# A planner's TensorE prices, per-head deadlines and a delay for cache rows, in a decoder layer with an expert layer

## The chip, the cores and the metric

One core of one Trainium2 chip runs the whole layer as one hand-written program. The metric is the device time of one execution in microseconds; the median of three runs of the kernel before is 3883.09 us (3873.05 to 3890.93).

Engines: PE is TensorE (matrix multiplies), PEld its weight loads, DVE VectorE, ACT ScalarE, POOL GpSimd, which here only issues indirect DMAs, and SP SyncE, which issues all other DMAs. Each engine takes its instructions in the order in which they stand in its program, and an instruction whose semaphore is not there yet holds all that stand behind it.

## What is computed

One layer of a decoder, in float32, for 1024 prompt tokens (eight tiles of 128) and 8 sample tokens with caches of 1024 earlier rows:

```python
q_a, k_a, v_a, q_b, k_b, v_b = project(x, pos, attn_norm, w_in)      # 1024 -> 2304, rope
o_a = banded_attention(q_a, k_a, v_a, sink)                          # 8 heads, window 128
o_b = combine_dilations(three dilated branches)                      # 8 heads
x = x + concat(rms_norm(o_a), rms_norm(o_b)) @ w_out
h = rms_norm(x, ffn_norm)
q = (h @ w_q).reshape(tokens, 8, 2, 128)                             # peer_ffn
s1, i1 = top_k(q[..., 0] . sub_keys, 16); s2, i2 = top_k(q[..., 1] . sub_keys, 16)
top_s, eid = top_k(all sums s1 + s2, 16)                             # 16 of 16384 experts per head
act = gelu(einsum('cd,chkd->chk', h, u[eid]))                        # gathered rows of peer_u
y = x + einsum('chk,chkd->cd', softmax(top_s) * act, v[eid])         # gathered rows of peer_v
```

The sample tokens attend to gathered cache rows. The caches, moved by one row, are outputs too. Each token needs 8 x 16 = 128 rows of `peer_u` and 128 of `peer_v`, of 4 KB each. That is 2048 gathers of 128 rows (512 KB) for the prompt, and it is most of what the kernel moves.

## The kernel before, in words

**Two kinds of work share the engines.** The base work is all that is dense: projection (`z`, `ze`, `zt`, `zv`), attention (`s`, `sm`, `se`, `p`, `pe`, `v`, `vd`, `vo`), norms, output projection (`o`, `ox`, `os`, `on`, `oh`, `ht`, `hv`), the query product and key scores of the expert layer (`q`, `qe`, `k`, `ke`), and the ranking of a head (`r0` to `r3`, `ge`, `gd`), where `r3` writes the 16 row numbers of a head to `idx` (L2084). The sample's attention has stages of its own: `smul` multiplies and reduces keys (L2122, L2124), twice for each of the 8 tokens, and `spv` multiplies values on PE (L1567 to L1569).

The other kind is the walk over the experts. It has 1058 places. At place p POOL gathers row number p of u for 128 tokens into a ring of four buffers (`u_ring`, L1350), and for the place 18 back (`LAG`) a row of v into another ring of four (`v_ring`, L1355). DVE takes the dot product of the u rows with h (L2204). After 16 places a head is complete: DVE and ACT make its 16 weights. A v row is then weighed and added up either on PE, where ACT first writes a diagonal matrix `diag` (L1832) and PE multiplies it with `v_ring` into `acc` (L1594), or on DVE (L2244). A ring's buffer is free when its dot product, or its weighing, is done. Places 0 to 1023 belong to the tiles 0 to 7, 128 each, and the head h of tile t starts at place 128 t + 16 h; the sample's 8 places come last.

**Groups.** Tiles are worked in groups (0), (1, 2), (3, 4), (5, 6), (7 and the sample). While a group is ranked, the next one is projected and attends; the output projection of a group lies between such phases. Weights stream through `wbuf`, four buffers of 1 MB, again for each group.

**The order of the work** is made when the program is built. `times_of(s)` gives each stage its engines and times in us. `merged` interleaves the queues of a phase by their summed times into one list, `BASE`. The class `Planner` then walks through time: it has the picks (dot, weigh and so on) and the stages of each engine in order, and takes at each step what can begin first. `ready_stage` says when a stage's inputs are there. `deadlines` gives each stage a place by which it is due (`by`): a stage that is due goes before a pick, one that isn't goes after. `load` and `send` choose for each v row whether PE or DVE weighs it. What comes out are only orders: `PLAN_OF` for PE, ACT and DVE, `PLAN_SP` for SP, and `ON_PE`. No time of the table is in the program itself; every wait is on a semaphore.

**SP and the sample's rows.** `sample_keys(r)` waits for the `smul` of token r - 1 and issues six DMAs into the one buffer (`s_k`, `s_kA`, `s_q`); `sample_values(r)` waits for the `spv` of r - 1 and issues four. So the rows of a token are asked for only when the token before is done.

Of the kernel before, what the change touches and what calls it, by code (L numbers as in the profile page):

```python
# [213 lines left out]
def pick_v(p):  # L214
    return pick_u(p - LAG) if p >= LAG else None
# [30 lines left out]
def times_of(s):  # L246
    kind, a, b = s[:3]
    sample = SAMPLE in (a, b) if kind in ("ze", "z") else a == SAMPLE
    n = a + 1 if kind in ("s", "sm", "se", "p", "pe", "v") else 0
    first = n == 1  # L250
    group = GROUPS[a] if kind in ("q", "qe", "k", "ke", "ge", "gd") else ()
    if kind == "z":
        return (("PE", 1.9 if a[0] == "kva" else 3.6),)
    if kind == "ze":
        return (("ACT", 0.7),) + ((("DVE", 1.7),) if a != "vb" else ())
    if kind == "o":
        return (("PE", 7.2),)
# [38 lines left out]
BASE = [s for phase in PHASES for s in merged(phase)]  # L296
AT = {s[:3] + tuple(s[6:7]): n for n, s in enumerate(BASE)}
# [95 lines left out]
ENGINES = ("PE", "ACT", "DVE")  # L393
HOP = 0.15
PACE = 2.9


class Planner:
# [51 lines left out]
    def deadlines(self):  # L450
# [4 lines left out]
        marks = [(self.given[0, 0], 0)]  # L455
        for t in ORDER[1:]:
            p = [p for p in range(PLACES) if pick_u(p) is not None and tile_of(pick_u(p)) == t][0]
            n = self.given[t, 0]
            if n > marks[-1][0]:
                marks.append((n, max(p - 10, 1)))  # L460

        total = [sum(cost[:n + 1]) for n, _ in marks]
        i = 0
        self.by = [0.0] * (marks[0][0] + 1)
        while i + 1 < len(marks):
# [5 lines left out]
            i = j  # L471
# [12 lines left out]
    def pick_line(self, e):  # L484

        out = []
        for p in range(PLACES):
# [9 lines left out]
            elif e == "ACT":  # L497
                out += [("tanh", ended, 0.3)] if ended is not None else []
                out += [("diag", p, 0.42)] if pick_v(p) is not None and pick_v(p)[0] == "f" else []
                out += [("fsq", final, 1.3)] if final is not None else []  # L500
            else:
                out += [("weigh", p, 1.98)] if pick_v(p) is not None else []
        return out

    def ready_stage(self, e):
# [3 lines left out]
        n, i, _ = self.parts[e][self.base[e]]  # L509
# [1900 lines left out]
```

How the kernel before makes its waits and increments, by code:

```python
        def need(eng, s, n):  # L777
            if n > 0:
                eng.wait_ge(s, n)
# [242 lines left out]
            def load_weights(b, i):  # L1023
                kind, g, part = W_LOADS[b][i]
                if i:
                    was, wg, wpart = W_LOADS[b][i - 1]
                    if was == "in":
                        sp.wait_ge(z_mm, Z_PARTS[wpart, IN_GROUPS[wg][-1]])
                    elif was == "out":
                        sp.wait_ge(o_mm, 2 * OI[GROUPS[wg][-1]] + wpart[0] + 1)
                    else:
                        sp.wait_ge(q_mm, 16 * wg + 2 * (wpart + 1))
                    if kind == "out" and g == LAST and part[0] == 0:
                        sp.wait_ge(s_fold, 1)
                if kind == "in":
                    c, half = part
                    w = COLS[c][1]
                    c0 = KD * sum(COLS[x][1] for x in CHUNKS[:CHUNKS.index(c)]) + 4 * w * half
                    sp.dma_start(wbuf[:, b, 0:4 * w], w_in[:, c0:c0 + 4 * w]).then_inc(wt_in[b], 16)
                elif kind == "out":
                    c0 = 4096 * part[0] + 2048 * part[1]
                    sp.dma_start(wbuf[:, b, :], w_out[:, c0:c0 + 2048]).then_inc(wt_in[b], 16)
                else:
                    sp.dma_start(wbuf[:, b, :], w_q[:, 2048 * part:2048 * (part + 1)]).then_inc(wt_in[b], 16)
# [14 lines left out]
            def load_x(kind, t):  # L1059
# [5 lines left out]
                    else:  # L1065
                        sp.wait_ge(o_h, OI[wt] + 1)
                        sp.wait_ge(x2_out[wt], 16)
                R = rows_of(t)
```

## Time and profile before

| | us |
|---|---|
| median of three runs | 3883.09 |
| lowest, highest | 3873.05, 3890.93 |
| the profiled execution | 3865.63 |
| its span, first to last instruction | 3863.8 |

| engine | busy us | share of the span |
|---|---|---|
| PE | 2715.3 | 70% |
| DVE | 2532.2 | 66% |
| POOL | 2339.2 | 61% |
| ACT | 631.4 | 16% |

The 16 DMA engines moved 1295.70 MB, of which the gathers are 1086.46 MB. No engine is full over the span, so what counts is where the DMA engines stand idle, and who let them. The profile is one execution, some 17 us shorter than the median of the runs.

### The profile page before, as it was taken

The numbers are of one execution on the slowest core, as the hardware profiler recorded it, in microseconds if no ns is written. First come the engines' busy times: TensorE is split into PE (matmuls) and PEld (weight loads), VectorE is DVE, ScalarE is ACT, GpSimd is POOL, SyncE is SP. The second block draws the span as 40 slices with busy tenths as digits, with TensorE's granted clock in tenths as the row PEclk, the third lists the DMA queues.
The fourth block names the chain that finished last, engine by engine and source line by source line (L and its number), as shares of the span: only waits on it lengthen the run. The fifth ranks groups of instructions, "written<-read, shape, count | busy, mean of one in ns | idle before, by whom it ended". The sixth has DMA issues, their size and how long they took to land.

```text
span 3863.8 us, 30640 instructions
## 1 busy us (share of the span) xinstructions
PE 2715.3 (70%) x7286; PEld 1323.9 (34%) x7286; DVE 2532.2 (66%) x6330; ACT 631.4 (16%) x1880; POOL 2339.2 (61%) x2076
## 2 busy tenths in 40 slices
PE   5866669687778777777798785457766566665665
PEld 3533335343434344334344343122332222222221
DVE  1467777677766677767667876555787555555553
ACT  2112212122211121212111121001111011110110
POOL 0155644476465577776745775444667777777774
PEclk7877879788899888888999888678987988888887
DMA  9799889899789899998988998777999999999997
GB/s 365 269 365 335 311 334 345 328 349 347 259 311 357 342 344 357 344 351 316 352 332 300 361 358 311 275 259 259 363 353 354 368 374 367 376 360 377 365 372 251
DMA packets 344554, 1295.70 MB, mean 335 GB/s; under 512 B 41880, under 2 KB 44784, under 8 KB 330912
## 3 DMA queue, kind: packets, MB, share of 16 engines
q0 software_dynamic: 298368, 1086.46, 76.2%
q1 hardware_dynamic: 46008, 207.29, 14.2%
q8 instruction: 61, 1.00, 0.1%
q14 instruction: 117, 0.96, 0.1%
HBM read 1272.76 MB, written 55.43 MB: 344 GB/s over the span
## 4 chain that ended last, share of the span: by engine, by line
POOL 24%; PE 24%; DMA 23%; issue 12%; DVE 9%; DVEq 3%; another core or an unknown queue 2%; ACT 1%; SPq 1%; ACTq 0%; POOLq 0%
DMA v_ring<-in_peer_v,idx 13%; POOL v_ring L1355 12%; POOL u_ring L1350 12%; PE acc L1594 12%; PE pS L1400 4%; DMA u_ring<-in_peer_u,idx 4%; PE pA L1526 3%; DMA wbuf<-zS_scr 2%; DVE u_ring L2204 2%; PE pS L1503 1%; DVE accs L2244 1%; DMA xbuf<-in_x_all 1%; PE pS L1442 1%; DMA o_all<-in_cache_swa 1%
## 5 line engine op out<-in xcount | busy, mean ns | idle before, releaser
L1594 PE MATMUL acc<-v_ring,diag 128*128 128x512 f32 x2820 | 1662.0, 733 | 861.0 <-DMA v_ring<-in_peer_v,idx 728.1
L1355 POOL DMA_INDIRECT v_ring<-in_peer_v,idx x1024 | 1191.3, 1163 | 772.3 <-PE acc L1594 355.4
L2204 DVE CUSTOM_DVE_ANT_0 u_ring<-u_ring,hb 128x1024 f32<-128x1024 f32 x1024 | 1244.7, 1222 | 577.8 <-DMA u_ring<-in_peer_u,idx 554.8
L1350 POOL DMA_INDIRECT u_ring<-in_peer_u,idx x1024 | 1123.5, 1097 | 713.3 <-issue 292.5
L1594 PEld LDWEIGHTS acc<-v_ring,diag 128*128 128x128 f32 x2820 | 605.5, 230 | 1748.6 <-issue 1603.1
L2244 DVE SCALAR_TENSOR_TENSOR accs<-v_ring,wv,accs 128x1024 f32<-128x1024 f32 x319 | 409.8, 1285 | 89.1 <-DMA v_ring<-in_peer_v,idx 57.4
L1832 ACT ACTIVATE diag<-idn,wv 128x128 f32<-128x128 f32 x705 | 264.8, 396 | 1160.1 <-PE acc L1594 818.9
L1400 PE MATMUL pS<-wbuf,T 128*128 128x512 f32 (+1 forms) x640 | 263.5, 562 | 22.7 <-DVE T L1927 16.0
L1526 PE MATMUL pA<-T,wbuf 128*128 128x256 f32 (+2 forms) x1280 | 256.4, 357 | 21.3 <-issue 15.6
L1526 PEld LDWEIGHTS pA<-T,wbuf 128*128 128x128 f32 x1280 | 221.2, 204 | 72.8 <-issue 46.6
L1400 PEld LDWEIGHTS pS<-wbuf,T 128*128 128x128 f32 x640 | 123.0, 197 | 142.7 <-issue 129.5
L1503 PE MATMUL pS<-wbuf,T 128*128 128x512 f32 (+1 forms) x288 | 131.4, 612 | 6.9 <-DVE xbuf L2000 4.4
L1442 PE MATMUL pS<-KTB,qT 64*128 64x512 f32 (+3 forms) x176 | 84.1, 591 | 58.2 <-DMA qT<-qT_scr 41.3
L1823 ACT ACTIVATE gl<-gl 128x16 f32<-128x16 f32 (+1 forms) x65 | 14.0, 215 | 642.7 <-DVE gl L2222 402.4
L1972 DVE CUSTOM_DVE_ANT_0 S<-pS,maskB 128x256 f32<-128x256 f32 (+6 forms) x56 | 46.2, 825 | 83.7 <-PE pM L1444 79.1
L1706 ACT ACTIVATE S<-S,anm 128x128 f32<-128x128 f32 (+7 forms) x64 | 49.5, 774 | 303.3 <-DVE anm L1979 248.9
L1479 PEld LDWEIGHTS pM<-VB,PT 128*128 128x128 f32 x560 | 79.5, 213 | 33.8 <-issue 22.4
L2204 DVE DVE_READ_ACCUMULATOR2_ANT dots<- 128x1 f32 x1024 | 84.1, 82 | 0.0
L1479 PE MATMUL pM<-VB,PT 128*128 128x64 f32 x560 | 78.2, 293 | 7.7 <-ACT PT L1642 6.7
L1503 PEld LDWEIGHTS pS<-wbuf,T 128*128 128x128 f32 (+1 forms) x288 | 53.2, 187 | 81.8 <-issue 81.8
L1941 DVE TENSOR_TENSOR onehot<-qT,rcs 128x64 f32<-128x64 f32 (+3 forms) x36 | 7.6, 212 | 102.2 <-ACT qT L1642 100.7
L1462 PE MATMUL pT<-idn,S 128*128 128x128 f32 x280 | 48.3, 311 | 36.8 <-ACT aden L1708 29.3
(224 smaller groups left out, 1908.4 us busy)
## 6 DMA issues: line engine op xcount, KB each, us to landing
wbuf<-in_w_in SPq DMA_DIRECT2D x40, 1024.0 KB
wbuf<-in_w_q SPq DMA_DIRECT2D x40, 1024.0 KB
out_dil_s<-in_cache_dil SPq DMA_DIRECT2D x8, 4092.0 KB
wbuf<-in_w_out SPq DMA_DIRECT2D x20, 1024.0 KB
u_ring<-in_peer_u,idx POOLq DMA_INDIRECT x1024
v_ring<-in_peer_v,idx POOLq DMA_INDIRECT x1024
xbuf<-in_x_all SPq DMA_DIRECT2D x16, 512.0 KB
wbuf<-in_w_in SPq DMA_DIRECT2D x10, 512.0 KB
```

The source lines that it names most:

```text
L1350: pool.indirect_dma_start(u_ring[:, entry % RU, :], None, table, bass.IndirectOffsetOnAxis(rows, 0))\
L1355: pool.indirect_dma_start(v_ring[:, entry % RV, :], None, peer_v, bass.IndirectOffsetOnAxis(rows, 0))\
L1400: m = pe.matmul(pS[0:R, 512 * (i % 2):512 * (i % 2) + w], xT[t][:, 4 * half + k, :], wbuf[:, b, k * w:(k + 1) * w], start=(half == 0 and k ...
L1442: pe.matmul(pS[:, b0 * P:b1 * P], qT[rows, q, 4 + p, :], KTB[rows, p, b0 * P:b1 * P], start=True, stop=True)
L1479: pe.matmul(pM[:, 0:64], PT[:, k, :], VB[:, k, cols], start=(k == 0), stop=(k == blocks_of(t) - 1))
L1503: m = pe.matmul(pS[0:R, half * 512:(half + 1) * 512], hT[g][:, k, columns(t)], wbuf[:, b, k % 4 * 512:(k % 4 + 1) * 512], start=(k == 0), ...
L1526: m = pe.matmul(pA[:, 0:width_of(GROUPS[g])], wbuf[:, b, k * 256 + i % 2 * P:k * 256 + (i % 2 + 1) * P], hT[g][:, k, :], start=(k == 0), s ...
L1594: m = pe.matmul(acc[0:R, half * 512:(half + 1) * 512], w, v_ring[:, entry % RV, half * 512:(half + 1) * 512], start=first, stop=last, skip ...
L1706: act.activation(B, B, ACT.Exp, bias=anm[:, b, 0:1], accum_out=aden[:, b, 0:1])
L1832: act.activation(diag[:, i % 4, :], idn[:, :], ACT.Copy, scale=wv[:, section % 2, v[1] % TOPK:v[1] % TOPK + 1]).then_inc(d_set, 1)
L2204: dve.tensor_tensor_reduce(row, row, hb[:, t % 2, :], 1.0, 0.0, ALU.mult, ALU.add, dots[:, section % 2, j:j + 1]).then_inc(u_used, 1)
L2244: dve.scalar_tensor_tensor(accs[:, i % 2, :], v_ring[:, e % RV, :], wv[:, section % 2, j:j + 1], accs[:, i % 2, :], ALU.mult, ALU.add).the ...
```

## The change

The diff touches the planner alone; no instruction of any engine has another form, and POOL issues the same gathers in the same order. It does five things.

1. `times_of`: the times of all PE stages are smaller, most of them by a factor of 1.1 to 2.8 (a product of the projection 3.6 to 2.0, of the output 7.2 to 4.0, of the queries of two tiles 4.0 to 2.1), and the weighing of a v row on PE goes from 1.98 to 1.25. Times of DVE and ACT stay.
2. `deadlines`: every head of a tile has its own mark; before, only head 0 of each tile had one.
3. `ready_stage`: a first part of `smul` and each `spv` can begin 12 us (`FETCH`) after the one before is done.
4. `ready_stage`: `r3` waits for the end of the tile that had the same `idx` slot.
5. `SLOTS`, `SLOT` and `width_of` are defined earlier.

```diff
@@ times_of @@
     if kind == "z":
-        return (("PE", 1.9 if a[0] == "kva" else 3.6),)
+        return (("PE", 1.1 if a[0] == "kva" else 2.0),)
...
-        "q": (("PE", 3.4 if len(group) == 1 else 4.0),), "qe": (("ACT", 0.36),), "k": (("PE", 0.45 * len(group)),),
+        "q": (("PE", 1.2 if width_of(group) < 2 * P else 2.1),), "qe": (("ACT", 0.36),), "k": (("PE", 0.2 * len(group) + 0.1),),
...
+FETCH = 12.0
...
@@ Planner.deadlines @@
-            n = self.given[t, 0]
-            if n > marks[-1][0]:
-                marks.append((n, max(p - 10, 1)))
+            for h in range(HEADS if t != SAMPLE else 1):
+                n = self.given[t, h]
+                if n > marks[-1][0]:
+                    marks.append((n, max(p + TOPK * h - 10, 1)))
...
@@ Planner.pick_line @@
-                out += [("weigh", p, 1.98)] if pick_v(p) is not None else []
+                out += [("weigh", p, 1.25)] if pick_v(p) is not None else []
...
@@ Planner.ready_stage @@
+        if BASE[n][0] in ("smul", "spv") and BASE[n][2] == 0:
+
+            m = n - 1 if BASE[n][0] == "spv" or BASE[n][1] == 0 else AT["smul", BASE[n][1] - 1, 1]
+            if BASE[n][0] == "spv" and BASE[n][1] == 0:
+                m = AT["smul", NS - 1, 1]
+            if BASE[n][0] == "spv" and BASE[n][1] > 0:
+                m = AT["spv", BASE[n][1] - 1, 0]
+            end = self.part_end.get((m, 0))
+            if end is None:
+                return None
+            ready = max(ready, end + FETCH)
+        if BASE[n][0] == "r3":
+
+            for t in BASE[n][6]:
+                if OI[t] >= SLOTS and ("fsum", ORDER[OI[t] - SLOTS]) not in self.ends:
+                    return None
```

In the changed kernel all lines below the planner stand 18 further down (L2204 is L2222, L1594 is L1612). Three places show what the new orders are.

**DVE, the sample's keys.** L2122 and L2124 are the multiply and reduce of `smul`, L2204 a dot product of the walk (two rows each), L2244 a weighing. Before, from the second part of one token's `smul` to the first part of the next:

```order
L2122 TENSOR_TENSOR wbuf<-o_all,wbuf 128x512
L2124 TENSOR_REDUCE PT<-wbuf 128x8
L2204 ISA u_ring,dots<-u_ring,hb 128x1024
L2204 ISA dots 128x1
L2244 SCALAR_TENSOR_TENSOR accs<-v_ring,wv,accs 128x1024
L2204 ISA u_ring,dots<-u_ring,hb 128x1024
L2204 ISA dots 128x1
L2122 TENSOR_TENSOR wbuf<-wbuf 128x1024
```

After, the end of such a stretch (it begins with one more dot product; L2102 writes the row numbers of a head):

```order
L2102 SCALAR_TENSOR_TENSOR idx<-sel 128x2x16
L2222 ISA u_ring,dots<-u_ring,hb 128x1024
L2222 ISA dots 128x1
L2262 SCALAR_TENSOR_TENSOR accs<-v_ring,wv,accs 128x1024
L2222 ISA u_ring,dots<-u_ring,hb 128x1024
L2222 ISA dots 128x1
L2222 ISA u_ring,dots<-u_ring,hb 128x1024
L2222 ISA dots 128x1
L2140 TENSOR_TENSOR wbuf<-wbuf 128x1024
```

Before, two places of the walk lie between one token's end and the next token's start (none to two in all such stretches); after, it is four to six. The sample's whole attention lies over the places 596 to 652 before and 452 to 561 after.

**DVE, the row numbers of head 5 of tiles 1 and 2**, of which POOL needs the first at place 208. L2084 writes them, L2217 closes the head before. Before:

```order
L2065 TENSOR_REDUCE sel<-onehot 128x32
L2084 SCALAR_TENSOR_TENSOR idx<-sel 128x2x16
L2089 TENSOR_REDUCE gsum<-gexp 128x2
L2091 RECIPROCAL gsum<-gsum 128x2
L2093 TENSOR_TENSOR gates<-gexp,gsum 128x2x16
L2204 ISA u_ring,dots<-u_ring,hb 128x1024
L2204 ISA dots 128x1
L2217 TENSOR_TENSOR gl<-dots 128x16
```

After, at the same closing of a head:

```order
L2083 TENSOR_REDUCE sel<-onehot 128x32
L2222 ISA u_ring,dots<-u_ring,hb 128x1024
L2222 ISA dots 128x1
L2235 TENSOR_TENSOR gl<-dots 128x16
L2236 SCALAR_TENSOR_TENSOR gl<-dots,gates 128x16
L2238 TENSOR_SCALAR gl<-gl 128x16
L2240 TENSOR_TENSOR gl<-gl,dots 128x16
```

Before, 208 dot products stand ahead of the write; after, 169 do, and the write is gone from here. For the heads 4 to 7, needed at the places 192, 208, 224 and 240, the writes stand behind 191, 208, 224 and 240 dot products before, and behind 144, 169, 191 and 211 after. The last head of all is ranked at place 746 before and at 643 after.

**PE, the projection of tiles 5 and 6.** L1400 x4 of 512 columns is one projection stage, L1526 x8 one query stage, L1416 a transpose, L1594 x2 one weighing. Before:

```order
L1400 MATMUL pS<-wbuf,T 128x512 x4
L1594 MATMUL acc<-v_ring,diag 128x512 x2
L1526 MATMUL pA<-T,wbuf 128x256 x8
L1400 MATMUL pS<-wbuf,T 128x512 x4
L1594 MATMUL acc<-v_ring,diag 128x512 x4
L1400 MATMUL pS<-wbuf,T 128x512 x4
L1594 MATMUL acc<-v_ring,diag 128x512 x2
```

After:

```order
L1612 MATMUL acc<-v_ring,diag 128x512 x4
L1418 MATMUL pS<-wbuf,T 128x512 x4
L1434 MATMUL pT<-idn,qT 128x128
L1544 MATMUL pA<-T,wbuf 128x256 x8
L1418 MATMUL pS<-wbuf,T 128x512 x4
L1434 MATMUL pT<-idn,qT 128x128
L1418 MATMUL pS<-wbuf,T 128x512 x8
L1612 MATMUL acc<-v_ring,diag 128x512 x2
```

Before, one or two base stages lie between weighings; after, five big ones do. Over the whole program PE weighs 713 v rows before and 789 after, DVE 319 and 243; of the first 120 places DVE weighs 54 before and 24 after.

## Rows read from the trace of the kernel before

**Rows 1.** Busy time by stretch, granted clock, DMA share and GB/s.

```profile
core 0: us, PE busy (x) PEld busy (x) DVE busy (x) ACT busy (x) POOL busy (x), PEclk, DMA share, GB/s
162.00:600.00 438.00, 298.45 (x993) 173.57 (x992) 315.06 (x878) 89.86 (x292) 225.73 (x200) 0.80 0.91 338
...
1200.00:1900.00 700.00, 538.48 (x1565) 279.19 (x1565) 513.42 (x1309) 140.45 (x407) 484.12 (x413) 0.88 0.93 342
...
2300.00:2760.00 460.00, 280.40 (x650) 118.50 (x651) 277.07 (x626) 51.92 (x159) 238.85 (x211) 0.77 0.82 293
...
2960.00:3760.00 800.00, 504.42 (x833) 184.54 (x834) 459.99 (x769) 83.02 (x230) 615.86 (x560) 0.84 0.98 368
```

**Rows 2.** u gathers issued in two stretches, counted: x, ns min/median/max, first and last.

```profile
L1350 POOL DMA_INDIRECT u_ring<-in_peer_u,idx x61: 932/938/1974, 2371.4 to 2683.7; - x61
...
L1350 POOL DMA_INDIRECT u_ring<-in_peer_u,idx x280: 933/937/2167, 2961.1 to 3759.9; - x140
```

**Rows 3.** The page: GB/s moved in each of 40 slices.

```profile
GB/s 365 269 365 335 311 334 345 328 349 347 259 311 357 342 344 357 344 351 316 352 332 300 361 358 311 275 259 259 363 353 354 368 374 367 376 360 377 365 372 251
```

**Rows 4.** POOL's waits over the span: us in total, times, longest.

```profile
POOL v_ring L1355 <- PE acc L1594: 366.1, 164, 24.4
...
POOL u_ring L1350 <- DVE idx L2084: 218.7, 5, 161.5
POOL u_ring L1350 <- DVE dots L2204: 202.0, 68, 14.0
POOL v_ring L1355 <- DVE accs L2244: 133.9, 35, 14.4
```

**Rows 5.** Around one token's keys: start, us, instruction, [idle before]; DVE, then SP.

```profile
2389.57 0.69 DVE L2124 TENSOR_REDUCE PT<-wbuf 128x8 f32<-128x512 f32 x1
...
2405.02 1.23 DVE L2122 TENSOR_TENSOR wbuf<-wbuf 128x1024 f32<-128x1024 f32 x1 [11.10 <-DMA wbuf<-zS_scr]
...
2392.91 0.65 SPq L1187 DMA_DIRECT2D wbuf<-zS_scr  x1
```

**Rows 6.** DVE's wait for the sample's keys over the span.

```profile
DVE wbuf L2122 <- DMA wbuf<-zS_scr: 70.6, 8, 12.7
```

**Rows 7.** POOL, the sample's stretch, the first and the last of nine.

```profile
2386.69 1.68 POOL L1355 DMA_INDIRECT v_ring<-in_peer_v,idx  x1 [14.40 <-DVE accs L2244]
...
2651.54 1.15 POOL L1355 DMA_INDIRECT v_ring<-in_peer_v,idx  x1 [21.98 <-PE acc L1594]
```

**Rows 8.** POOL in order of time, where it lacked row numbers.

```profile
983.95 0.94 POOL L1350 DMA_INDIRECT u_ring<-in_peer_u,idx  x1 [19.08 <-DVE idx L2084]
...
1048.53 0.94 POOL L1350 DMA_INDIRECT u_ring<-in_peer_u,idx  x1 [19.59 <-DVE idx L2084]
...
1107.26 0.94 POOL L1350 DMA_INDIRECT u_ring<-in_peer_u,idx  x1 [13.19 <-DVE idx L2084]
```

**Rows 9.** The page's group of DVE's weighings.

```profile
L2244 DVE SCALAR_TENSOR_TENSOR accs<-v_ring,wv,accs 128x1024 f32<-128x1024 f32 x319 | 409.8, 1285 | 89.1 <-DMA v_ring<-in_peer_v,idx 57.4
```

**Rows 10.** PE's groups by shape: records, busy us, mean ns, idle before.

```profile
L1594 PE MATMUL acc<-v_ring,diag 128*128 128x512 f32 x2820 | 1662.0, 733 | 861.0 <-DMA v_ring<-in_peer_v,idx 728.1 <-ACT diag L1832 86.6 <-issue 45.2
L1400 PE MATMUL pS<-wbuf,T 128*128 128x512 f32 x512 | 230.4, 599 | 6.7 <-DMA wbuf<-in_w_in 4.2 <-ACT qT L1642 2.4
L1526 PE MATMUL pA<-T,wbuf 128*128 128x256 f32 x768 | 184.5, 395 | 6.8 <-issue 3.7 <-ACT sc L1642 3.1
L1503 PE MATMUL pS<-wbuf,T 128*128 128x512 f32 x256 | 117.3, 615 | 6.9 <-DVE xbuf L2000 4.4 <-ACT T L1642 2.5
...
L1513 PE MATMUL pT<-idn,S 128*128 128x128 f32 x64 | 11.1, 332 | 25.2 <-DVE S L2010 25.2
```

**Rows 11.** Two stretches with the granted clock, as in rows 1.

```profile
200.00:400.00 200.00, 125.59 (x427) 75.50 (x428) 140.29 (x406) 45.88 (x158) 106.16 (x97) 0.74 0.91 339
...
1200.00:1300.00 100.00, 91.59 (x247) 45.82 (x248) 72.45 (x210) 15.78 (x40) 56.20 (x48) 0.97 0.95 361
```

More of the change, by code:

```diff
@@ L41 @@
 SC_SLOTS = 4
+SLOTS = 5
+SLOT = {t: i % SLOTS for t, i in OI.items()}
 PLACE_IN_GROUP = {t: s for g in GROUPS for s, t in enumerate(g)}
@@ L68, in rows_of, with width_of @@
     return NS if t == SAMPLE else P
+def width_of(group):
+    return sum(rows_of(t) for t in group)
 def prompt_of(group):
@@ L260, in times_of @@
     return {
-        "xg": (("DVE", 2.7),), "zt": (("PE", 0.5 if a == "kva" else 1.8),),
+        "xg": (("DVE", 2.7),), "zt": (("PE", 0.3 if a == "kva" else 0.8),),
         "zv": (("ACT", 0.35 if a == "kva" else 0.65),),
-        "s": (("PE", 0.8 if first else 0.6 + 0.25 * n),), "sm": (("DVE", 1.9 if first else 1.3 + 0.14 * n),),
-        "se": (("ACT", 1.4 if first else 1.3 + 0.12 * n),), "p": (("PE", 0.9 if first else 0.8 + 0.4 * n),),
-        "pe": (("ACT", 0.5 if first else 0.9 + 0.12 * n),), "v": (("PE", 0.7 if first else 0.7 + 0.3 * n),),
+        "s": (("PE", 0.6 if first else 0.6 + 0.13 * n),), "sm": (("DVE", 1.9 if first else 1.3 + 0.14 * n),),
@@ L266, in times_of @@
+        "se": (("ACT", 1.4 if first else 1.3 + 0.12 * n),), "p": (("PE", 0.6 if first else 0.5 + 0.18 * n),),
+        "pe": (("ACT", 0.5 if first else 0.9 + 0.12 * n),), "v": (("PE", 0.5 if first else 0.5 + 0.14 * n),),
         "vd": (("DVE", 0.6),), "vo": (("ACT", 0.6),),
-        "n1": (("ACT", 1.5),), "n2": (("DVE", 2.9),), "n3": (("ACT", 1.3),), "nt": (("PE", 3.3),), "ng": (("ACT", 2.4),),
+        "n1": (("ACT", 1.5),), "n2": (("DVE", 2.9),), "n3": (("ACT", 1.3),), "nt": (("PE", 1.6),), "ng": (("ACT", 2.4),),
@@ L272, in times_of @@
         "ge": (("ACT", 0.3),), "gd": (("DVE", 0.9),),
-        "sin": (("DVE", 2.2),), "smul": (("DVE", 2.7 if b == 0 else 1.6),), "ssc": (("PE", 1.6),),
-        "ssm": (("DVE", 2.6),), "sse": (("ACT", 1.2),), "ssd": (("DVE", 1.5),), "spr": (("PE", 1.5),),
-        "spe": (("ACT", 1.0),), "spv": (("PE", 2.4),), "sod": (("DVE", 2.0),), "sfo": (("PE", 1.8),),
+        "sin": (("DVE", 2.2),), "smul": (("DVE", 2.7 if b == 0 else 1.6),), "ssc": (("PE", 1.0),),
+        "ssm": (("DVE", 2.6),), "sse": (("ACT", 1.2),), "ssd": (("DVE", 1.5),), "spr": (("PE", 1.0),),
@@ L276, in times_of @@
+        "spe": (("ACT", 1.0),), "spv": (("PE", 2.1),), "sod": (("DVE", 2.0),), "sfo": (("PE", 1.1),),
         "so": (("DVE", 1.3),), "sr0": (("DVE", 3.4),), "sr1": (("DVE", 2.4),), "sr2": (("DVE", 1.5),), "sr3": (("DVE", 2.7),), "sge": (("ACT", 0.3),),
@@ L714 @@
 STAGED = {x: i for i, x in enumerate(x for x in Z_ITEMS if x[0] in ("qa", "qb") and 0 < x[1] < NT)}
-SLOTS = 5
-SLOT = {t: i % SLOTS for t, i in OI.items()}
 R3 = [s for s in BASE if s[0] == "r3"]
 RANKED = {(t, s[2]): i + 1 for i, s in enumerate(R3) for t in s[6]}
-def width_of(group):
-    return sum(rows_of(t) for t in group)
 X_LOADS = (("sq", 0), ("sq", 1), ("sq", 2), ("o", 0), ("sq", 3), ("sq", 4), ("o", 1), ("o", 2), ("sq", 5), ("sq", 6),
```

4 lines of the change are left out of this document (2 added, 2 removed).

## The prediction, as it was put on record

> **What bounds the kernel now.** I read the GB/s of the slices first, then busy time by stretch, then what POOL waited for, since POOL issues the gathers that are most of the traffic. From 2960 us on, when all base work is over, the DMA engines are busy for 0.98 of the time at 368 GB/s [rows 1], and 280 places pass in 800 us, 2.857 us each [rows 2]. That stretch is bound by DMA alone, and no order of the engines can shorten it. Earlier the same engines move 338, 342 and, around the sample's attention, 293 GB/s [rows 1]; the slices show the same dip, 311 275 259 259 [rows 3]. The bytes are the same whatever the order. So the kernel's time is its bytes at about 368 GB/s plus the time in which the DMA engines are starved, and POOL's waits tell who starves them: PE's weighings, DVE's dot products and weighings, and row numbers that come late [rows 4]. It follows that moving base work to earlier places is worth nothing by itself: a place that goes without base work later costs its 2.857 us all the same. Only starved time can be won, and only new starved time can be lost.
>
> **Part 1, the sample's cache rows.** In the order before, at most two places lie between the end of one token's `smul` and the start of the next. The trace shows what the rows take: the reduce ends at 2390.26, SP's last request goes out at 2392.91, and the next multiply begins at 2405.02 after 11.10 us of idling on DVE [rows 5]; 14.8 us from end to start. Over eight tokens DVE idles 70.6 us for them [rows 6], dot products and weighings stand behind it, both rings fill, and POOL pauses. Nine such pauses of over 6 us, from the first to the last shown [rows 7], add up to 122.7 us; the last two are PE waiting for the value rows in the same way. What is it worth? The places 600 to 660 took 312 us [rows 2]. Undisturbed they cost 60 x 2.857 = 171 us, and the sample's own rows, some 13 MB, another 13/0.368 = 36 us. 312 - 171 - 36 = 105 us starved. By rates instead: 460 us at 293 GB/s are 135 MB, 394 us at the 342 of the stretch 1200 to 1900 [rows 1], a gain of 66 us. After the change four to six places lie between, 11.4 to 17.1 us at 2.857, against the 14.8 measured; SP's order has nothing new in between. Some stretches will still be short by up to 3 us, which a ring of four buffers (11.4 us) swallows. I take **-95 us**, bounds -105 to -66.
>
> **Part 2, deadlines per head.** Before, the numbers of the heads 5, 6 and 7 of tile 1 are written on DVE only after all the dot products that stand before them, and POOL, which runs ahead of DVE, waits 19.08, 19.59 and 13.19 us for them [rows 8], 51.9 us. The first of the five waits of that kind, 161.5 us [rows 4], is the start of the kernel and stays: 136 instead of 138 base stages stand ahead of it. After the change 28 places or more lie between a head's write and its need, from head 0 of tile 1 on. The gain can't be more than 51.9 us; in the slices there the rate is 259 and 311 [rows 3], so some traffic of SP used the gaps. I take **-45**, bounds -52 to -32.
>
> **Part 3, more weighings on PE.** 76 go from DVE to PE, 30 of them in the first 120 places. That takes 30 x 1.285 = 39 us [rows 9] from a DVE that is busy for 315 of the first 438 us [rows 1]. There POOL waits for DVE more than for PE. On PE a weighing has 4 records: 1662.0/705 = 2.36 us [rows 10], and 30 x 2.36 = 71 us come in where PE is busy for 298 of 438. I take **-15**, bounds -39 to 0. In the places without base work DVE has room and this is worth nothing.
>
> **Part 4, PE's new prices.** Counted by stage, the trace gives 230.4/64 = 3.6 us for a projection stage (8 records), 184.5/48 = 3.84 for a query stage (16), 117.3/16 = 7.3 for half an output product (16), and 11.1/8 = 1.4 for the eight transposes of a tile [rows 10]. The old table has 3.6, 4.0, 7.2 and 3.3, the new one 2.0, 2.1, 4.0 and 1.6. So the new table is right for transposes, and for products it has little more than half of what this trace shows; a weighing is 1.25 against 2.36, or 1.7 with the clock at its upper level. The planner therefore lays product stages on PE closer than they fit. In the rows of PE's order five big stages stand between two weighings: 3.6 + 3.84 + 3.6 + 7.2 and two small transposes, 18.7 us. Four v buffers cover 4 x 2.857 - 1.7 = 9.7 us; behind that POOL stops. Priced so, 18 stretches between weighings exceed the cover, by 98 us together, nearly all at three spots where one group's output product meets the next projection (places 80 to 120, 200 to 240, 360 to 400). Before, 9 such stretches exceeded it, by 26 us, and one long stretch in which DVE did the weighing. But DMA has weights to load at these spots, so starved time is less: over 80 to 119, 200 to 239 and 360 to 399 PE has 215, 212 and 222 us of work, DMA 193, 193 and 189 (40 places at 2.857 and the weights), an excess of 74 us; before, it was 8. A dense PE also gets its higher clock, 0.97 at 92% busy against 0.74 in the stretch 200 to 400 [rows 11], so the stages there cost some 5% less than the mean. I take **+45**, bounds 0 to +98.
>
> **Part 5, between these spots.** From place 240 to 360 and 400 to 440 the base work of PE rises by some 5 us in 20 places (57 us), DVE's stays. PE was 77% busy in 1200 to 1900 [rows 1] and would be near 85%. I take **+10**, bounds 0 to +40. The `r3` rule for `idx` slots binds nowhere near: the tiles in question end over 100 places before the write.
>
> A page of the notes speaks on part 4: the Trainium skill, "Perfetto Trace Analysis", section "Tensor Engine Instruction (MATMUL, LD_WEIGHTS)", says that a matmul's recorded end is estimated from its size and not observed. If PE's records overstate, the new table may be nearer the truth; that is the second rival. Against it stands that busy time per stage counts back-to-back records by their starts, not by the last end.
>
> **The sum.** 3865.6 (the profiled execution) - 95 - 45 - 15 + 45 + 10 = 3765.6. The median of the runs is 17.5 us above the profiled execution, so 3783.
>
> **Rivals.** (a) *The delay is too short.* 12 us stands against 14.8 measured, and SP's requests queue behind gathers. If half of part 1 stays, 3783 + 48 = 3831. For it: five places at 2.857 are 14.3 us. Against it: a miss of 1 to 3 us, not 11, and rings that cover it. (b) *PE's prices are good enough.* Parts 4 and 5 cost nothing, parts 1 to 3 give -95 - 52 - 25: 3865.6 - 172 + 17.5 = 3711. For it: PE stands idle 728 us waiting for v rows [rows 10], room that a dense order could use. Against: that idling lies elsewhere. (c) *PE becomes the bound and the kernel slower.* The place is the three spots; the price is each stretch between weighings that outlasts 9.7 us. The 18 hold 273 us of stages; at the clock of 0.74 instead of some 0.86 they hold 317, 142 more than their cover. With +40 of part 5 and gains of only 66 and 32: 3865.6 + 142 + 40 - 98 + 17.5 = 3967. It decides once the uncovered time passes the 98 to 155 us of gains. Against it speaks the clock that rises with density. (d) *The two cancel*: the orders change as planned, and what is won at the sample is lost at the spots, about 3883. That the delay or the deadlines did nothing is excluded by the orders themselves.
>
> **Chances.** Forecast 0.55, (b) 0.17, (a) 0.11, (d) 0.07, (c) 0.10. A difference of 0.5%, 19 us, is about what measurements of this kernel can tell. Faster by more: the first three, less a little for (a) with less gain elsewhere, 0.80; within 0.10; slower 0.10. The range 3700 to 3880 leaves out (c), most of (d) and the best ends of all bounds at once.
>
> **What would show it.** Part 1: DVE's wait for the keys under 25 us and no POOL pause over 6 us from the sample's rows, the dip to 259 gone. Part 2: no wait of POOL for `idx` but the first. Part 3: shorter waits of POOL for DVE before 600 us. Part 4: POOL's wait for PE's `acc` grows, with pauses of 5 to 10 us bunched at three spots, and PE over 90% busy there. The stretch without base work must still show 2.857 us a place. The prediction is wrong if the DMA rate outside the sample's part falls below that of before, or if new waits of DVE for PE's results stand in front of dot products.

## The result and the profile after

The changed kernel took 3931.86 us (median of 4 runs, 3921.03 to 3942.17) where the kernel before, run beside it, took 3878.14: a ratio of 1.0133, 95% interval 1.0093 to 1.0173. It is slower by some 52 us; the forecast was 100 us faster. The profiled execution has a span of 3919.2 us.

The page's GB/s in 40 slices, which answer to [rows 3]; three holes have replaced the old dips:

```profile
GB/s 362 263 316 347 301 298 262 320 314 343 341 274 191 339 350 360 354 282 212 306 353 370 374 368 386 282 313 348 368 368 368 365 369 366 371 359 377 357 372 258
```

Busy time by stretch, columns as in [rows 1]. The first three lines are the places 80 to 119, 220 to 239 and 360 to 399, the fourth the places 200 to 219, the fifth the places 402 to 525 with the sample's keys, the last the stretch without base work:

```profile
475.00:732.00 257.00, 210.40 (x669) 116.49 (x668) 148.13 (x491) 53.19 (x146) 87.51 (x80) 0.91 0.78 280
1079.00:1269.00 190.00, 147.23 (x486) 86.20 (x485) 90.52 (x329) 34.03 (x86) 41.87 (x41) 0.87 0.67 234
1651.00:1894.00 243.00, 207.21 (x625) 102.63 (x623) 140.47 (x445) 43.29 (x114) 83.29 (x80) 0.91 0.73 255
...
1011.00:1079.00 68.00, 57.06 (x146) 25.61 (x144) 52.37 (x135) 13.25 (x38) 47.88 (x41) 0.95 0.93 331
...
1900.00:2300.00 400.00, 281.78 (x719) 131.28 (x720) 302.31 (x690) 67.72 (x193) 281.29 (x248) 0.85 0.98 361
...
2960.00:3760.00 800.00, 508.78 (x852) 183.24 (x852) 447.16 (x737) 85.66 (x236) 595.64 (x557) 0.85 0.98 367
```

The same places 80 to 119, 200 to 239 and 360 to 399 in the kernel before:

```profile
455.00:655.00 200.00, 155.19 (x470) 86.06 (x471) 143.69 (x409) 34.71 (x96) 93.74 (x82) 0.87 0.90 335
...
941.00:1107.00 166.00, 120.55 (x394) 66.53 (x393) 125.32 (x361) 38.84 (x123) 89.47 (x80) 0.85 0.77 281
1545.00:1668.00 123.00, 94.60 (x289) 50.88 (x288) 95.04 (x236) 30.36 (x88) 92.37 (x80) 0.85 0.95 347
```

The stretch without base work is unchanged (367 GB/s against 368). The three spots took 257 + 258 + 243 = 758 us instead of 200 + 166 + 123 = 489, 269 more. By the times at which POOL issues its u gathers, the rest of the walk took less: the places 120 to 200 and 240 to 360 lost 7 and 55 us, 400 to 580 lost 51, 580 to 660 lost 83 and 660 to 1020 lost 35, while the first 80 took 21 us more. The sum is some 58 us. What was gained at the sample and what came back for base work moved ahead did not pay for the spots. By the rows above not all of the 269 us is starved time. Time times GB/s gives 201 MB moved in the three spots after and 156 before: some 45 MB, mostly the weights of base work that now stands there, are 121 us at 368 GB/s, and other places no longer have to move them. Time times the idle share of DMA gives 191 us starved after and 64 before, 127 more. The two make 248 of the 269. Both are estimates from rounded rows of one execution each.

POOL's waits over the span, which answer to [rows 4] (us in total, times, longest):

```profile
POOL v_ring L1373 <- PE acc L1612: 483.1, 193, 18.6
POOL u_ring L1368 <- DVE dots L2222: 342.0, 78, 15.4
...
POOL u_ring L1368 <- DVE idx L2102: 160.5, 1, 160.5
...
POOL v_ring L1373 <- DVE accs L2262: 25.4, 19, 3.2
```

DVE's wait for the sample's keys, which answers to [rows 6]:

```profile
DVE wbuf L2140 <- DMA wbuf<-zS_scr: 6.5, 4, 2.9
```

So the change did at its own places what it should: row numbers are waited for only at the start (218.7 us in five waits, now 160.5 in one), the sample's keys cost 6.5 us instead of 70.6, and waiting for DVE's weighings falls from 133.9 to 25.4. But waiting for PE's weighings grew by 117 us and for DVE's dot products by 140. Pauses of POOL over 6 us, without the first wait for row numbers, add up to 437 us (42 of them; before, 350 in 30), and 311 us of them (29 pauses) lie in the three spots.

What holds DVE's dot products up shows in DVE's own waits, for the x rows and for PE's attention scores (`pM`). Before, then after:

```profile
DVE S L1972 <- PE pM L1444: 79.1, 21, 15.3
...
DVE xbuf L2000 <- DMA xbuf<-in_x_all: 6.9, 1, 6.9
```

```profile
DVE S L1990 <- PE pM L1462: 135.3, 32, 15.5
...
DVE xbuf L2018 <- DMA xbuf<-in_x_all: 61.8, 4, 18.6
```

**Inside one spot.** The chain of waits through the places 220 to 239 shows three parts (start, us, what; x is a count of records):

```profile
1083.98 15.37 DMA xbuf<-in_x_all
1099.38 1.23 DVE xbuf L2018
...
1107.26 1.30 DVE S L2028
1108.60 1.97 PE pT L1531 x8
...
1111.79 6.11 PE pA L1544 x16
1117.90 1.72 PE acc L1612 x4
...
1174.40 1.72 PE acc L1612 x4
1176.11 3.43 PE pS L1418 x8
...
1179.99 10.30 PE pS L1418 x24
1190.29 3.45 PE pA L1544 x16
1193.75 1.72 PE acc L1612 x4
...
1218.94 5.90 DMA qT_scr<-qT
1224.90 5.88 DMA qT<-qT_scr
1230.82 2.93 PE pS L1460 x4
...
1239.82 3.36 PE acc L1612 x4
```

The same three parts by busy time:

```profile
1083.00:1108.00 25.00, 5.60 (x20) 2.57 (x18) 7.43 (x19) 2.81 (x6) 5.81 (x6) 0.70 0.82 319
1111.00:1218.00 107.00, 105.73 (x337) 61.94 (x338) 58.55 (x221) 18.57 (x44) 21.21 (x21) 0.97 0.73 252
1218.00:1268.00 50.00, 29.41 (x109) 17.76 (x107) 20.13 (x78) 11.55 (x33) 10.46 (x9) 0.76 0.44 144
```

First, 28 us in which the end of one group's output product stands in a row: DVE waits for the x rows, adds them, normalizes, PE transposes, and only then can the queries begin. Then 107 us in which PE is 99% busy with projection, queries and weighings. Last, 50 us of attention, with a round trip of q through memory (11.8 us) and then PE, DVE and ACT by turns; the DMA engines are busy for 0.44 of it. In all three, dot products and weighings stand in line behind other stages, and POOL has no free buffer. PE and DMA don't idle in the same parts. PE idles for some 20 us in the entry and 21 in the attention and for 1 in between. The DMA engines idle for 5 us in the entry, where the x rows come behind two blocks of weights, for 29 in the dense part and for 28 in the attention.

### The profile page after: what moved, and what is told of

It reads as the page before. It is cut to its first block, busy times and chain, and to the rows that moved or that the text cites. A ratio compares the mean times of both kernels' runs of the same rounds, so it can differ in the third digit from the quotient of the medians.

```text
span 3919.2 us, 31248 instructions
## 1 busy us (share of the span) xinstructions
PE 2815.0 (72%) x7590; PEld 1347.1 (34%) x7590; DVE 2433.2 (62%) x6254; ACT 664.2 (17%) x1956; POOL 2275.0 (58%) x2076
## 4 chain that ended last, share of the span: by engine, by line
PE 30%; POOL 23%; DMA 19%; issue 14%; DVE 7%; DVEq 2%; ACT 2%; another core or an unknown queue 1%; SPq 0%; ACTq 0%; POOLq 0%
PE acc L1612 13%; POOL v_ring L1373 12%; POOL u_ring L1368 11%; DMA v_ring<-in_peer_v,idx 11%; PE pS L1418 6%; PE pA L1544 4%; PE pS L1521 3%; DMA xbuf<-in_x_all 2%; DMA u_ring<-in_peer_u,idx 2%; DVE u_ring L2222 2%; DMA wbuf<-zS_scr 1%; PE pS L1460 1%; DMA wbuf<-in_w_in 1%; DVE accs L2262 1%
## 5 line engine op out<-in xcount | busy, mean ns | idle before, releaser
L1612 PE MATMUL acc<-v_ring,diag 128*128 128x512 f32 x3124 | 1780.1, 712 | 780.6 <-DMA v_ring<-in_peer_v,idx 668.7
L2222 DVE CUSTOM_DVE_ANT_0 u_ring<-u_ring,hb 128x1024 f32<-128x1024 f32 x1024 | 1244.9, 1223 | 663.3 <-DMA u_ring<-in_peer_u,idx 617.0
L1373 POOL DMA_INDIRECT v_ring<-in_peer_v,idx x1024 | 1163.8, 1136 | 814.4 <-PE acc L1612 475.7
L1368 POOL DMA_INDIRECT u_ring<-in_peer_u,idx x1024 | 1086.3, 1061 | 795.3 <-DVE dots L2222 342.0
L1612 PEld LDWEIGHTS acc<-v_ring,diag 128*128 128x128 f32 x3124 | 650.7, 224 | 1767.7 <-issue 1652.1
L1850 ACT ACTIVATE diag<-idn,wv 128x128 f32<-128x128 f32 x781 | 296.0, 397 | 1307.4 <-PE acc L1612 760.1
L2262 DVE SCALAR_TENSOR_TENSOR accs<-v_ring,wv,accs 128x1024 f32<-128x1024 f32 x243 | 312.3, 1285 | 65.3 <-DMA v_ring<-in_peer_v,idx 35.4
L1418 PE MATMUL pS<-wbuf,T 128*128 128x512 f32 (+1 forms) x640 | 261.5, 558 | 20.3 <-DVE T L1945 15.4
L1990 DVE CUSTOM_DVE_ANT_0 S<-pS,maskB 128x256 f32<-128x256 f32 (+6 forms) x56 | 46.2, 825 | 150.4 <-PE pM L1462 135.3
L1497 PE MATMUL pM<-VB,PT 128*128 128x64 f32 x560 | 73.4, 280 | 19.9 <-ACT PT L1660 11.1
L2222 DVE DVE_READ_ACCUMULATOR2_ANT dots<- 128x1 f32 x1024 | 84.5, 83 | 0.0
L2018 DVE TENSOR_TENSOR xbuf<-xbuf,pS 128x1024 f32<-128x1024 f32 (+1 forms) x9 | 11.0, 1220 | 104.0 <-DMA xbuf<-in_x_all 61.8
```

Source lines behind the costliest of these rows:

```text
L1368: pool.indirect_dma_start(u_ring[:, entry % RU, :], None, table, bass.IndirectOffsetOnAxis(rows, 0))\
L1373: pool.indirect_dma_start(v_ring[:, entry % RV, :], None, peer_v, bass.IndirectOffsetOnAxis(rows, 0))\
L1418: m = pe.matmul(pS[0:R, 512 * (i % 2):512 * (i % 2) + w], xT[t][:, 4 * half + k, :], wbuf[:, b, k * w:(k + 1) * w], start=(half == 0 and k ...
L1497: pe.matmul(pM[:, 0:64], PT[:, k, :], VB[:, k, cols], start=(k == 0), stop=(k == blocks_of(t) - 1))
L1612: m = pe.matmul(acc[0:R, half * 512:(half + 1) * 512], w, v_ring[:, entry % RV, half * 512:(half + 1) * 512], start=first, stop=last, skip ...
L1850: act.activation(diag[:, i % 4, :], idn[:, :], ACT.Copy, scale=wv[:, section % 2, v[1] % TOPK:v[1] % TOPK + 1]).then_inc(d_set, 1)
```

## The experiments

Times are compared by ratio to the kernel before in runs of the same chip, since that kernel took 3845.55, 3831.14 and 3882.15 us in the three sets. The ratios and intervals are those on record; they differ from the quotient of the two medians by up to 0.4% (fetch_only: 0.986 against 0.982). Differences between two ratios are good to 0.5 to 1 per cent.

**times_only: the new PE prices alone, in the kernel before.** They take the place of the old ones in `times_of` and `pick_line`; deadlines and delay stay as they were.

```diff
-        return (("PE", 1.9 if a[0] == "kva" else 3.6),)
+        return (("PE", 1.1 if a[0] == "kva" else 2.0),)
...
-                out += [("weigh", p, 1.98)] if pick_v(p) is not None else []
+                out += [("weigh", p, 1.25)] if pick_v(p) is not None else []
```

> The kernel before with only the new PE prices (stages and weighing); marks of head 0 alone, no delay for cache rows. Theory A, the new prices squeeze base work into a few spots and the squeeze is what costs: the loss is all here and the gain at the sample is missing, so about 3932 + 95 = 4027 us, 3980 to 4060, with places 80 to 120 and one later pair of projections at 5 to 9 us a place, and POOL pauses at the sample's rows as before. Rival B, the prices are harmless and deadlines or delay did the harm: 3850 to 3890.

Measured: 3951.89 us, ratio 1.030 (1.0221 to 1.0379). The prices alone make the kernel slower, by more than the whole change. On the scale of the first chip the ratio is 3994 us, in the range of theory A, though only 1.6% (some 65 us) above the changed kernel where 95 were expected. The three spots took 265, 249 and 253 us. Its slices show the spots in new places and the sample's stall, which nothing cured here (228 to 293):

```profile
GB/s 358 266 332 339 310 283 261 302 285 329 336 305 192 340 355 329 361 277 191 326 357 293 251 228 291 370 367 379 377 376 373 369 370 396 406 378 386 387 390 270
```

**old_times: the changed kernel with all old PE prices.** The reverse edit in the changed kernel; per-head deadlines, delay and the `r3` rule stay.

> The changed kernel with the old PE prices (stages and weighing); deadlines per head, delay and idx rule stay. Theory A: the gains of parts 1 and 2 without the squeeze, 3878 - 95 - 45 = 3738 us, 3715 to 3780; no stretch of 20 places over 6 us a place. Rival B: about 3932, 3900 to 3950.

Measured: 3726.95 us, ratio 0.972 (0.9645 to 0.9796). The prices are therefore worth 1.0133/0.972 = 1.042, or 160 us, in the changed kernel, and all that the change cost comes from them. No 20 places, counted in twenties from 0, took over 5.9 us each. Waiting for v rows to be weighed fell from 483.1 to 396.3 us, for dot products from 342.0 to 201.1, and the places 220 to 239 took 62 us (columns as in [rows 1]):

```profile
1028.00:1090.00 62.00, 51.30 (x129) 22.56 (x129) 49.39 (x140) 12.89 (x39) 45.21 (x41) 0.92 0.93 341
```

**fetch_only and heads_only: each cure alone, in the kernel before.**

```diff
+FETCH = 12.0
...
+            ready = max(ready, end + FETCH)
```

> The kernel before with only the delay of 12 us for the sample's keys and values. Theory A: part 1 alone, 3878 - 95 = 3783 us, 3773 to 3812 by its bounds; DVE's wait for the keys falls from 70.6 us to under 25. If half of the stall stays because the rows take 14.8 us and not 12: about 3830. If the DMA engines were not starved there at all: 3878.

Measured: 3774.74 us, ratio 0.9857 (0.9784 to 0.9929).

```diff
+            for h in range(HEADS if t != SAMPLE else 1):
+                n = self.given[t, h]
...
+                    marks.append((n, max(p + TOPK * h - 10, 1)))
```

> The kernel before with only a mark per head in the deadlines. Theory A: part 2 alone, 3878 - 45 = 3833 us, 3826 to 3846; POOL's waits for idx are gone but the first. If the time in those waits was used by other traffic: 3865 to 3880.

Measured: 3817.69 us, ratio 0.9934 (0.9895 to 0.9972). By the times, each fell between its theory A and the rival value (0.973 to 0.983 and about 0.988 for fetch_only, 0.987 to 0.992 and 0.997 or more for heads_only). By the traces each removed its own wait and left the other. fetch_only, POOL's and DVE's waits:

```profile
POOL u_ring L1362 <- DVE idx L2096: 223.2, 5, 161.0
...
DVE wbuf L2134 <- DMA wbuf<-zS_scr: 8.3, 4, 2.8
```

heads_only, the same two waits:

```profile
POOL u_ring L1351 <- DVE idx L2085: 161.7, 2, 161.4
...
DVE wbuf L2123 <- DMA wbuf<-zS_scr: 88.2, 8, 14.0
```

Alone they give 1.4% and 0.7%, together 2.8%. The surplus of 0.7% lies within the intervals, so the times alone don't show that it is more than the sum; the traces, of one chip, show how it can be. At place 580 heads_only stood at 2265 us and fetch_only at 2326: 61 us ahead. From 580 to 680, where the sample's attention lies in both, heads_only then took 487 us and fetch_only 327. Against the kernel before, whose trace is of another chip, heads_only was 48 us ahead at place 580 and 3 at place 680: its lead was used up in the sample's stall. In old_times most of the lead of the deadlines is kept (2284 at place 580, 334 us to 680). Against each other in spans, the delay on top of the deadlines is worth 3822.1 - 3732.5 = 90 us (83 by the ratios), the deadlines on top of the delay 3766.6 - 3732.5 = 34 us (53 by the ratios). The first lies close to the 95 forecast, the second on either side of 45.

**old_stages and old_weigh: which of the new prices does it.** In the changed kernel, old_stages has the stage times of the old table and 1.25 for a weighing; old_weigh has the new stage times and 1.98 for a weighing.

```diff
-                out += [("weigh", p, 1.25)] if pick_v(p) is not None else []
+                out += [("weigh", p, 1.98)] if pick_v(p) is not None else []
```

> The changed kernel with the stage times of the old table; a weighing on PE stays priced at 1.25, and the delay and the marks stay. It ranks the last head at place 742 (changed kernel: 643) and weighs 768 rows on PE (789). Theory S, the small prices of the base stages do the harm, since they pack base work into three spots where PE, ACT and DVE wait for one another: ratio to the kernel before 0.97 to 0.985, no 20 places over 7 us each, most of the way back to the 0.972 of old_times. Rival W, the price of a weighing does it, since more rows are weighed on PE and fewer on DVE: ratio 1.00 to 1.015, as the changed kernel, with long waits of POOL for PE's acc spread over all places with base work.

> The changed kernel with a weighing on PE priced at 1.98 again; the new small stage times, the delay and the marks stay. It ranks the last head at place 648 (changed kernel: 643) and weighs 763 rows on PE (789). Theory S (stage prices do the harm): ratio to the kernel before 1.005 to 1.02, with the places 220 to 240 at 8 us or more each. Rival W (the weighing's price does it): ratio 0.97 to 0.985. If both prices share the harm, this one and old_stages both land near 0.99.

Measured: old_stages 3718.79 us, ratio 0.9684 (0.9641 to 0.9726), no 20 places over 6.2 us each; old_weigh 3853.02 us, ratio 1.0064 (1.0025 to 1.0103), the places 220 to 239 at 8.3 us each. Theory S stands: the stage prices cost 1.0133/0.9684 = 1.046, the weighing's price 1.0133/1.0064 = 1.007, at the edge of what the two intervals tell. The traces put this last part at the start: the first 80 places took 293 us before, 314 in the changed kernel, 310 in times_only, and 297 and 293 in old_weigh and old_stages, so it takes both small prices. In orders that are spread out the 63 more weighings on PE (768 against 705) go with a ratio 0.4% lower, about 14 us, which these intervals can't tell from nothing.

**traced: PE prices as the trace of the kernel before shows them.** In the changed kernel (three of the changed lines; the other PE times and the weighing's 2.0 as in the expectation):

```diff
-        return (("PE", 1.1 if a[0] == "kva" else 2.0),)
+        return (("PE", 2.1 if a[0] == "kva" else 3.6),)
...
-        return (("PE", 4.0),)
+        return (("PE", 7.3),)
...
-FETCH = 12.0
+FETCH = 15.0
```

> The changed kernel with PE times as the trace of the kernel before shows them: projection stage 3.6 (kva 2.1), half an output product 7.3, query stage 3.84 (2.25 for one tile), transposes of a tile 1.4, s 0.7 + 0.24 n, v 0.6 + 0.28 n, a weighing 2.0, and a delay of 15 us. It ranks the last head at place 763. Theory S: with prices that fit what PE shows the planner leaves room for the chain of engines: ratio to the kernel before 0.965 to 0.975, equal to old_times or up to 0.7% faster, no 20 places over 6.5 us each. Rival D, the new deadlines pack the work and the prices hardly matter: 0.99 or more.

Measured: 3710.34 us, ratio 0.9664 (0.9616 to 0.9712). So it isn't new prices that hurt but small ones: prices taken from the trace are as good as the old ones, and no better within the intervals. (The delay went to 15 us in the same run, so the two aren't told apart here.)

**half_proj and half_proj_old: is PE full at the spots?** Both leave half of the projection's product out; q, k and v are therefore those of half the contraction. half_proj is made from the changed kernel, half_proj_old from old_times.

```diff
-                for k in range(4):
+                for k in range(2):
...
-                                  stop=(half == 1 and k == 3), skip_group_check=True)
+                                  stop=(half == 1 and k == 1), skip_group_check=True)
```

> The changed kernel with half of the projection's product left out: each projection stage on PE does 2 of its 4 blocks of the contraction (4 records of 512 columns instead of 8, some 1.7 us instead of 3.4); orders, transfers and all other stages stay. It tells what bounds the three spots. Theory P, PE is full there (99% busy from 1111 to 1218 us in the changed kernel): the places 220 to 240, 190 us with 64 us of projection records in them, take 150 to 165 us, the three spots together give back 70 to 100 us, ratio to the kernel before 0.985 to 0.995 (changed kernel 1.0133). Rival C, latency of the chain PE, ACT, DVE bounds the spots and PE's amount of work doesn't: the places 220 to 240 take 180 us or more, ratio 1.005 to 1.013.

> The same half of the projection's product left out of old_times (the changed kernel with the old PE times), as the control: the same PE work goes, but from orders in which it is spread. Theory P: PE is seldom full there, so little comes back, 0 to 25 us, ratio to the kernel before 0.965 to 0.972 (old_times 0.972). If PE work were worth its time everywhere, some 110 us would come back here too, and the ratio would be near 0.945.

Measured: half_proj 3871.32 us, ratio 0.9958 (0.9927 to 0.999); half_proj_old 3731.03 us, ratio 0.9621 (0.9582 to 0.966). In half_proj the places 220 to 239 took 171 us instead of 190, and the three spots gave back 49 us (690 to 641, with 220 to 239 counted for the second): between what the two theories expected. Its chain of waits through the same spot:

```profile
1061.46 15.64 DMA xbuf<-in_x_all
...
1089.55 5.17 PE pA L1544 x16
...
1177.88 6.85 DMA qT_scr<-qT
1184.78 5.61 DMA qT<-qT_scr
1190.43 2.93 PE pS L1460 x4
```

and busy time of its parts:

```profile
1090.00:1190.00 100.00, 78.08 (x258) 46.49 (x257) 58.73 (x219) 18.25 (x43) 24.78 (x24) 0.91 0.85 305
1190.00:1228.00 38.00, 29.03 (x109) 17.90 (x110) 19.50 (x77) 11.65 (x35) 5.82 (x7) 0.80 0.28 85
```

From the first query product to the round trip of q it takes 88 us (1089.55 to 1177.88), 107 in the changed kernel (1111.79 to 1218.94): all of the 19 us won lie here. PE's projection records fell by 27 us in the places 220 to 239, so not all of that came back; with less work PE waits in this part too (78 us busy of the 100 shown). The entry (28 us, from the request for the x rows) and the attention (50 us) are as long as before. So both theories hold, each for its part of the spot: 107 us of the 190 are bound by PE, 78 by transfers and stages that wait for one another, whatever PE has to do; 5 us lie ahead of the entry. In the control less came back: 1.0% against 1.75% by the ratios, and 10 us against 50 in the three times 40 places by the traces (456 to 446 us, 758 to 708). The 1.0% is 38 us where at most 25 were expected, but the intervals leave both open. How much of the 78 us would be covered if the same stages stood farther apart wasn't tried by itself; that old_times has no such hole says that most of it is. Nor was it tried to ask for the x rows ahead of the two blocks of weights. DVE's wait for them is 61.8 us in the changed kernel and 62.8 in half_proj, 41.9 in times_only and 40.3 in old_weigh, but at most 16.7 in every run with the old or the traced stage prices.

**old_fetch16, old_fetch20 and stages_fetch16: is the delay too short?** old_times with `FETCH` at 16 and 20, old_stages with 16.

```diff
-FETCH = 12.0
+FETCH = 16.0
```

> old_times (the changed kernel with all old PE times) with the delay for the sample's rows at 16 us instead of 12. Theory F, 12 us against 14.8 measured is covered by the rings: ratio within 0.4% of the 0.972 of old_times, and no pause of POOL over 6 us goes in the sample's part. Rival (a), the delay is too short: 0.960 to 0.967, since DVE's remaining wait for the keys goes away.

> old_times with the delay at 20 us (12: 0.972, 16: 0.965). If the rows still came late at 16: 0.958 to 0.963. If 16 covers the 14.8 us measured and more only drags the sample's attention out: 0.964 to 0.970.

> old_stages (the changed kernel with the old stage times and the new 1.25 for a weighing, 0.968) with the delay at 16 us. If the 0.7% that 16 us gave in old_fetch16 is real and adds up: 0.960 to 0.964, the fastest so far. If it was scatter between chips or between orders: 0.966 to 0.970.

Measured: old_fetch16 3705.79 us, ratio 0.9648 (0.9597 to 0.9698); old_fetch20 3741.53 us, 0.9645 (0.961 to 0.968); stages_fetch16 3770.89 us, 0.9709 (0.9666 to 0.9752). DVE's wait for the keys from `wbuf` is 11.8 us at 12, and at 16:

```profile
DVE wbuf L2140 <- DMA xbuf<-zS_scr: 3.8, 1, 3.8
...
DVE wbuf L2140 <- DMA wbuf<-zS_scr: 0.4, 1, 0.4
```

The wait goes as it should, but it was small. old_fetch16 came out at the number of rival (a), its sister stages_fetch16 the other way; the intervals overlap with those of 12. The three comparisons give 0.7% and 0.7% for more than 12 us and 0.2% against it, and the waits that went (15.3 us of waiting for keys at 12, 4.2 at 16) are 0.3%; a gain stays open. old_fetch16, old_fetch20 and traced are the fastest versions, some 3.5% below the kernel before, and not told apart from one another nor from old_stages.

## Why the prediction was wrong

- **Part 1** (95 us forecast): right where the deadlines are also in place, 90 us by the spans and 83 by the ratios; alone 1.4%, about 55. After the change DVE waits 6.5 us for keys (under 25 expected), the new stretch of the sample's keys moves 361 GB/s, and no pause over 6 us is left there. In fetch_only the stall itself is gone, 259 us for the places 580 to 659 instead of 371 (traces of two chips). It took 628 us from place 680 to 880 where heads_only took 580, but at 363 and 367 GB/s: these are transfers that were still due, and no new stall. Why its ratio shows only 55 us isn't settled by a run.
- **Part 2** (45): right with the delay in place, 34 to 53 us, and the four waits for row numbers are gone, as expected. Alone it showed only 0.7%, since part of its lead was lost in the sample's stall.
- **Part 3** (15): waits for DVE's weighings went down as expected (133.9 to 25.4 us), and before 600 us POOL waited 116 us for DVE instead of 143. But it waited 60 us for PE there instead of 22, and the first 80 places took 21 us more and not less: there the sign was wrong. In the spread-out orders of old_stages the gain is 0.4% at most, within its error.
- **Parts 4 and 5** (45 + 10): here the forecast failed. With part 3 the prices were put at +40; measured they are +160. The places were right and so was PE's work in them: 215, 212 and 222 us were forecast for the three times 40 places, 210, 204 and 207 were there. The place and the sign were rival (c)'s. The step that failed is the one that set the time of a spot to the larger of PE's work and DMA's. The time was 257, 258 and 243, that is 47, 54 and 36 us above PE's own work, because the dense part has an entry and an attention at its ends in which PE waits too, while the DMA engines idle in the dense part and the attention. That is shown in one spot, the places 220 to 239, and taken over to the other two. The starved time, for which I had 74 us and took 45, is (1 - 0.78) x 257 = 57, 0.07 x 68 + 0.33 x 190 = 68 and 0.27 x 243 = 66, together 191 us, against 64 at the same places before (20, 38 and 6). The 127 more and the 21 us of the first 80 places come to 148, near the measured 160. A second error was the width: work and traffic were added up over the places 200 to 239, while the order packs 147 us of PE work into the last 20, which no transfer of the first 20 can use. Part 5 had its reading the wrong way round: between the spots, over the places 240 to 359 and 400 to 439, PE's work without weighings fell from 198 to 141 us instead of rising by 57. The places 240 to 359 took 382 us instead of 438 at an unchanged rate (347 GB/s against 348), since the projection and its weights had moved into the spots.
- **The discount for the clock** went the right way and was too small to matter: 0.97 in the dense part, but 0.76 in the attention behind it, after PE had idled 12.5 us.
- **The signs that were named** came true for the worse: the rate fell at the spots (280, 259 and 255 GB/s over the three times 40 places, against 335, 281 and 347), and new waits for PE stand in front of dot products (135.3 us against 79.1). PE was 99% busy in the dense part looked at; over the three times 40 places it was 82, 79 and 85%.
- **What bounds the stretch without base work** was taken for a constant, 2.857 us a place, that no order can shorten. The changed kernel kept it (278 gathers in 800 us, 2.88). But from place 840 to 1000 times_only took 2.70 us a place and heads_only 2.80 on one chip, at a DMA share of 1.00 and 0.99. What sets this rate isn't shown by any run.
- **Rival (b)**, the small prices being nearer the truth, falls. The new price of a projection stage was 2.0; in the spot 24 of its records follow one another in 10.30 us, 3.43 us a stage, from start to start at 0.97 of full clock, so no end of a record enters. A weighing took 1.72 there, not 1.25. The Trainium skill, "Perfetto Trace Analysis", section "Tensor Engine Instruction (MATMUL, LD_WEIGHTS)", says that recorded ends are estimated; that holds nothing against a price read from starts, and the summed busy time that I used (3.6) was within 5% of it.
- **Rival (a)** falls as far as it can be told, and the cancelling of **(d)** was nearer than the forecast, but what cancelled was 109 us against 160.
- **Rival (c)** was priced at 3967 and given 0.10. It came nearest in time, but not for its reason: it had PE as the bound at a clock of 0.74, and the spots ran at 0.91, 0.87 and 0.91, with PE the bound in 107 of the 190 us looked at. It was set low because of PE's rising clock and because DMA has weights to load at the spots. Neither bears on the parts that are bound by turns. A chain that was left out should have raised its chance, since the last line of [rows 10] already shows PE idle for 25.2 us before 11.1 us of transposes, waiting for DVE.

## What to carry to other kernels

When a planner's prices fall below what the trace shows, what to add up is not the work of the fullest engine: look in the new order for the stretch where the dependent stages stand side by side, and add to the engine's work the transfers and hand-overs at its ends, for with nothing between them the engines wait in turn. Ask of each part what DMA does in it: the entry above was long but hardly starved. Compare prices with start-to-start times of back-to-back records before trusting a table. Two cures on the same path should be measured together and alone, for a gain made ahead of a stall may be lost in it.

## What the runs showed of the hardware

- One weighing on PE (4 records of 512 columns, float32) took 1.72 us between dense stages, at a granted clock of 0.97 in that part (1.00 is the upper level, 2.4 GHz). It took 3.36 and 3.56 us at 1239.82 and 1249.94 us, after a pause of 12.5 us of the same engine that ended at 1230.82; from 1231 to 1240 us the granted clock is 0.50, the lower level of 1.2 GHz. At 1261.07 us one took 1.77 again.
- 512 KB of x rows, asked for right behind two blocks of 1 MB of weights and a store of 512 KB, took 15.4 us in a spot, and one way of q's round trip 5.9 us.
- The kernel before took 3831 to 3882 us (medians) on the chips of these runs. From 3150 to 3550 us, where no run has base work left, the kernel before and the changed kernel moved 369 and 367 GB/s, and the runs of the three other chips 371 to 387, 369 to 388 and 361 to 367, all at a DMA share of 0.97 to 1.00. So chips differ, and so do the runs of one chip.
